# Three edits to a hybrid decoder-layer kernel: an earlier plain load, two other PSUM banks, and a norm in two parts

## The chip, the cores and the metric

The kernel runs on one core of a Trainium2 chip. The core has five engines that work side by side and wait for one another through semaphores: TensorE (PE, matmuls; its weight loads are shown as PEld), VectorE (DVE), ScalarE (ACT), GpSimd (POOL) and SyncE (SP, which issues transfers). Matmul results go to PSUM, which has 8 banks of 512 float32 columns on 128 partitions; everything else lies in SBUF. The metric is the device time of one execution, in microseconds (us). Each engine works its instructions off in order; a wait at the head of its queue holds back all that is behind it.

## The reference

One layer of a decoder is computed for a prompt of 1024 tokens and for 8 sample tokens with a paged cache. What matters here is branch B and the MLP:

```
h = RMSNorm(x);  z = h @ w_in                     # pool channels, q1 q2, k1 k2, v, gates
q, k = rope(q), rope(k)                           # 8 heads, two maps of 64 channels each
s = q k^T / 8, masked;  p = softmax(s)            # for each of the two maps
o = (p[0] - lam * p[1]) @ v                       # per head, 128 x 128 per token block
o = RMSNorm_head(o) * (1 - lam_init)
merged = gate_pool * (pool_out @ w_pool_proj) + gate_attn * (o @ w_attn_proj)
x = x + merged @ w_o
x = x + square(relu(RMSNorm(x) @ w_up)) @ w_down
y = RMSNorm(x)
```

All is float32; the kernel splits each operand of a large product into a high and a low part (`_hi`, `_lo`) and sums three products of those.

## The kernel before, in words

There is no scheduler: the order on each engine is written out, and semaphores are counted.

**Heads.** The 8 heads are pipelined. `head(h, ...)` exists once for each engine and runs nine steps s = 0 to 8 (NTT = 8 token blocks and one for the samples). In step s, TensorE computes the scores of block s of head h (`scores`, L853), sums the values of block s-2 (`values`, L895), projects token block s of the *next* head with one third each of q, k, v (`project`, L836, in two halves of 12 matmuls; the samples' one, s = 8, is L825 to L829), transposes the weights of block s-1 (`weight_transposes`, L885) and turns q and k of block s-1 of the next head (`qk_transposes`, L845 and L846, called the turn). ScalarE takes the exponentials (L1361) and copies the high parts out of PSUM (L1368, L1346, L1374); VectorE takes the maxima (L1837), weighs (L1847 to L1852), takes the low parts (L1859, L1829), applies the rotary factors and frees the projection's bank (`rotate`, L1821 to L1825), and makes the low halves of the next weights (`split_qkv`, L1780). POOL finishes the rotary sums (L2526, L2527) and raises the variances to the power -1/2 (`rstd_head`, L2542).

**Banks.** Projections use bank 0, only blocks 1 and 8 (the samples) use bank 3; both bank 3 and bank 5 are the second halves of the scores' two maps, used from block 4 on. The turn uses bank 6, which the weights' transposes of blocks 4 to 7 use too. So turn 7 waits until VectorE has read the last transposed weights out of bank 6 (`s_atlo`), and the projection of block 0 of the head after waits until the samples' projection has been read (`z_before`, `s_zfree`), though it writes another bank.

**Norm.** In step 1 of the next head VectorE waits for the squares of head h-1, writes `o_var` (L1870), waits for POOL's `o_rstd` and multiplies the whole head with it (L1872), and only then goes on to the low part of block 0 (L1859). The normed head is transposed in step 3 (`out_transposes`, L904).

**The last head** has no projection beside it; parts of the first product after the heads (`first_tile`, L1026, and `first_product`, L931) fill in from step 3 on.

**Down projection.** It runs in four spans of 28 blocks (4 pairs of 7 products); a block of the last span has 2 k-tiles (12 matmuls of 258 columns, L1171), the others 4. A table says at which block of a span each of the next span's seven inputs is loaded by ScalarE's queue (`NEXT_LOAD_AT`, L1598) and at which two blocks it is split (`NEXT_SPLIT_AT`; high part on ScalarE L1605, low part on VectorE L2335). After the last span comes `last_half`, products of one more input, the plain half (number PLAIN, `ff_plain_scratch`, twice the bytes of the others in the last span), which by the same table is loaded at block 6 of the last span and split at blocks 9 and 11. VectorE also makes the weights' low parts (L2189), the weights' sums (L2202 to L2208) and the additions into x (L2348, L2356), of which some free the accumulators in which TensorE goes on.

Of the kernel before, what the change touches and what calls it, by code (L numbers as in the profile page):

```python
# [18 lines left out]
NTT = SEQ // P  # L19
NCH = 3  # L20
CH = TOK // NCH
HEADS = 8
# [61 lines left out]
FIRST_SPLIT_AT = ((111, 112), (113, 114), (115, 116), (117, 118), (119, 120), (121, 122), (123, 124))  # L84
NEXT_LOAD_AT = (6, 12, 22, 23, 24, 25, 26)
NEXT_SPLIT_AT = ((9, 11), (15, 18), (25, 26), (26, 27), (28, 29), (30, 31), (32, 33))
Y_AT = {2: 8, 4: 7, 6: 6, 8: 5, 10: 4, 12: 3}
# [6 lines left out]
def need(eng, sem, value):  # L94

    if isinstance(value, int) and value <= 0:
        return
    eng.wait_ge(sem, value)


def decoder_layer(nc, ins, outs):
# [209 lines left out]
    with ExitStack() as ctx:  # L311
# [84 lines left out]
        def z_of(hp, t):  # L396

            if hp == 0:
                return first_z(t)
            return ps[:, 3] if t in (1, NTT) else bank_z  # L400

        def z_before(hp, t):

            before = {0: 0, 1: 0, 2: 1, NTT: 2}.get(t, t)
            return 9 * hp + before

        VS = 2
# [133 lines left out]
        for c in range(PLAIN + 1):  # L541
            g, i = divmod(c, W_BLOCKS)
            before = DOWN + W_BLOCKS * PER * (g - 1)
            load_at[c] = before + NEXT_LOAD_AT[i] if g else FIRST_LOAD_AT[i]
            split_at[c] = [before + k for k in NEXT_SPLIT_AT[i]] if g else FIRST_SPLIT_AT[i]

        def acc_a(p):
# [249 lines left out]
        def _(pe):  # L797
# [12 lines left out]
            def project(hp, t, half):  # L810
# [3 lines left out]
                if half == 0:  # L814
                    need(pe, s_zfree, z_before(hp, t) if hp else t - 1)
                    if hp and t == NTT:
                        pe.wait_ge(s_exp, 16 * hp)
                if hp and t == NTT:
                    if half == 0:
# [28 lines left out]
            def scores(h, par, i):  # L848

                pe.wait_ge(s_qklo, 8 * h + i + 1)  # L850
                need(pe, s_exp, 16 * h + 2 * (i - 1 if h == HEADS - 1 and 2 <= i <= 3 else i))
# [85 lines left out]
            def head(h, par, proj, normed):  # L937

                def turn_qk(t):

                    if t == 0:
                        need(pe, s_atlo, 12 * h)
                    elif t >= 4:
                        pe.wait_ge(s_atlo, 12 * h + ROUNDS[t] + 2)
                    else:
                        pe.wait_ge(s_qklo, 8 * (h + 1) + t)
                    if t == 2 and normed:
                        pe.wait_ge(s_one, 2 * h - 1)
                    qk_transposes(h + 1, 1 - par, t)

# [360 lines left out]
        def _(act):  # L1311
# [79 lines left out]
            def head(h, par, proj, normed):  # L1391
                if proj:
                    split_qkv(h + 1, (2, 3) if normed else (0, 1, 2, 3))
                for s in range(NTT + 1):
# [23 lines left out]
                    if proj and s >= 1:  # L1418
                        qk_high(h + 1, 1 - par, s - 1)
                    if proj and s == NTT:  # L1420
# [354 lines left out]
        def _(dve):  # L1775
# [91 lines left out]

            def normed_head(h, par):
                dve.wait_ge(s_oq, 8 * h + 8)
                dve.tensor_scalar(o_var[:], ssq[:, par], 1.0 / DH, SUBLN_EPS, ALU.mult, ALU.add).then_inc(s_ovar, 1)  # L1870
                dve.wait_ge(s_orstd, h + 1)
                dve.tensor_tensor(o_st[:, par], o_st[:, par], o_rstd[:].unsqueeze(2).to_broadcast([P, NTT, P]),  # L1872
                                  ALU.mult).then_inc(s_on, 1)

            def head(h, par, proj, normed, k_par):
                if proj:
                    split_qkv(h + 1, (2, 3) if normed else (0, 1, 2, 3))
                for s in range(NTT + 1):
# [5 lines left out]
                    if normed and s == 1:  # L1884
                        normed_head(h - 1, 1 - par)
                    if s >= 2:
# [18 lines left out]
                    if proj and s >= 1:  # L1905
                        qk_low(h + 1, 1 - par, s - 1)

# [75 lines left out]
            key_products(0)  # L1983
            o_sum(HEADS - 1, 1, NTT - 1)
            normed_head(HEADS - 1, 1)
            for s_ in s_kv:
# [639 lines left out]
```

## Time and profile before

| | us |
|---|---|
| median of 3 runs | 1711.28 (1711.20 to 1712.22) |
| the profiled execution's own time | 1712.73 |
| its span, first to last instruction | 1710.7 |
| busy: PE / DVE / ACT / POOL | 1667.7 / 1188.4 / 736.9 / 133.7 |
| mean granted TensorE clock | 0.993 of full |

The profile is of one execution. Busy times overlap between engines. In rows of the timeline a bracket gives how long the engine had been idle before the row, and what ended it; the ends of matmuls are modelled, so that the distance from start to start tells more than the idle time of PE.

### The profile page before, as it was taken

Reading aid. Unit: us, or ns where it says so; the run is one execution under the profiler, and the core shown is the slowest. Engines: PE = TensorE matmul, PEld = TensorE weight load, DVE = VectorE, ACT = ScalarE, POOL = GpSimd, SP = SyncE. Lnnn points to the kernel's source line nnn. Section 1 sums busy time; section 2 is a strip of 40 time slices with the busy share of each in tenths; the row PEclk is TensorE's granted clock in tenths of the full one; section 3 lists DMA queues with packets and bytes.
Section 4 is the critical chain, followed back from the end, with each engine's and each line's share of the span. In section 5 each row is a group of like instructions: output and inputs, shape, how many; then the busy total and the mean of one; then the engine's idle time right before and its main releaser. Section 6 shows DMA issues by size and latency. Waiting matters only on the chain.

```text
span 1710.7 us, 30509 instructions
## 1 busy us (share of the span) xinstructions
PE 1667.7 (97%) x12112; PEld 1614.6 (94%) x12112; DVE 1188.4 (69%) x1978; ACT 736.9 (43%) x1512; POOL 133.7 (8%) x244
## 2 busy tenths in 40 slices
PE   7999999999989999999999999999999999999988
PEld 7889889889878999999999999999999999999987
DVE  6677777777776788765444458777676786868686
ACT  4455555555554321265311345334433553544343
POOL 3212212222210000000000000000000000000001
PEclk9999999999999999999999999999999999999999
DMA  6202202201213527665412222444444733444223
GB/s 205 63 2 75 63 16 72 75 23 54 69 32 104 182 93 229 204 216 173 142 50 62 75 87 66 158 148 154 138 136 137 280 123 119 155 157 137 92 75 125
DMA packets 153212, 195.22 MB, mean 114 GB/s; under 512 B 7785, under 2 KB 121385, under 8 KB 151016
## 3 DMA queue, kind: packets, MB, share of 16 engines
q1 hardware_dynamic: 138352, 160.56, 29.4%
q10 hardware_dynamic: 14720, 32.72, 5.3%
q8 instruction: 97, 1.59, 0.4%
q14 instruction: 43, 0.35, 0.1%
HBM read 149.35 MB, written 44.13 MB: 113 GB/s over the span
## 4 chain that ended last, share of the span: by engine, by line
PE 89%; DVE 6%; issue 2%; ACT 2%; DMA 1%; POOL 0%; DVEq 0%; ACTq 0%; POOLq 0%
PE ps L1171 34%; PE ps L931 23%; PE ps L836 16%; PE ps L862 3%; PE ps L895 3%; PE ps L885 2%; PE ps L1224 1%; PE ps L1281 1%; PE ps L1078 1%; DVE kv_pages L1962 1%; DVE w_lo L1780 1%; PE ps L866 1%; DVE mx L1837 1%; PE ps L806 0%; DMA d_raw<-ff_plain_scratch 0%
## 5 line engine op out<-in xcount | busy, mean ns | idle before, releaser
L836 PE MATMUL ps<-w_hi,h_hi 128*128 128x384 f32 x520 | 182.3, 351 | 4.7 <-DVE w_lo L1780 2.7
L836 PE MATMUL ps<-w_hi,h_lo 128*128 128x384 f32 x520 | 176.8, 340 | 0.0
L836 PE MATMUL ps<-w_lo,h_hi 128*128 128x384 f32 x520 | 176.0, 338 | 0.0
L1171 PE MATMUL ps<-d_hi,m_hi 128*128 128x258 f32 x784 | 158.8, 284 | 5.3 <-DVE m_lo L2189 2.6
L1171 PE MATMUL ps<-d_lo,m_hi 128*128 128x258 f32 x784 | 159.2, 285 | 0.0
L1171 PE MATMUL ps<-d_hi,m_lo 128*128 128x258 f32 x784 | 158.2, 283 | 0.0
L1361 ACT ACTIVATE prob<-ps,nbias 128x256 f32<-128x256 f32 (+7 forms) x128 | 94.9, 742 | 84.8 <-DVE nbias L1840 82.4
L1171 PEld LDWEIGHTS ps<-d_hi,m_hi 128*128 128x128 f32 x784 | 121.6, 190 | 6.0 <-DVE x L2356 3.0
L1171 PEld LDWEIGHTS ps<-d_hi,m_lo 128*128 128x128 f32 x784 | 122.4, 190 | 0.0
L1171 PEld LDWEIGHTS ps<-d_lo,m_hi 128*128 128x128 f32 x784 | 121.8, 190 | 0.0
L1578 ACT ACTIVATE m_hi<-m_pair 128x512 fp32r<-128x512 f32 (+1 forms) x128 | 76.9, 600 | 104.3 <-PE ps L1171 91.5
L2189 DVE TENSOR_TENSOR m_lo<-m_pair,m_hi 128x512 fp32r<-128x512 f32 (+1 forms) x128 | 83.9, 655 | 50.6 <-ACT m_hi L1578 49.4
L1578 ACT ACTIVATE m_hi<-m_sum 128x512 fp32r<-128x512 f32 (+1 forms) x96 | 57.8, 602 | 112.1 <-PE ps L1171 85.0
L836 PEld LDWEIGHTS ps<-w_hi,h_hi 128*128 128x128 f32 x520 | 97.7, 188 | 7.4 <-DVE kv_st L1825 3.3
L1171 PE MATMUL ps<-t_hi,m_hi 128*128 128x258 f32 x512 | 104.0, 285 | 0.0
L1171 PE MATMUL ps<-t_lo,m_hi 128*128 128x258 f32 x512 | 103.8, 284 | 0.0
L1171 PE MATMUL ps<-t_hi,m_lo 128*128 128x258 f32 x512 | 103.8, 284 | 0.0
L931 PE MATMUL ps<-h_hi,w_hi 128*128 128x344 f32 x456 | 99.0, 326 | 3.7 <-DVE w_lo L1979 1.7
L1837 DVE TENSOR_REDUCE mx<-ps 128x1 f32<-128x256 f32 (+7 forms) x128 | 96.0, 750 | 7.6 <-PE ps L866 7.6
L1464 ACT ACTIVATE w_hi<-w_raw 128x1024 fp32r<-128x1024 f32 x42 | 44.4, 1057 | 129.5 <-PE ps L931 117.0
L836 PEld LDWEIGHTS ps<-w_lo,h_hi 128*128 128x128 f32 x520 | 98.1, 189 | 0.6
L836 PEld LDWEIGHTS ps<-w_hi,h_lo 128*128 128x128 f32 x520 | 97.5, 188 | 0.7
(295 smaller groups left out, 4335.7 us busy)
## 6 DMA issues: line engine op xcount, KB each, us to landing
ff_combination_scratch<-ff_st SPq DMA_DIRECT2D x14, 1806.0 KB, 6.9
d_raw<-ff_combination_scratch ACTq DMA_DIRECT2D x21, 1032.0 KB, 7.9
w_raw<-in_w_in SPq DMA_DIRECT2D x41, 512.0 KB, 5.3
kv_pages<-in_cache_k SPq DMA_DIRECT2D x32, 512.0 KB, 5.3
kv_pages<-in_cache_v SPq DMA_DIRECT2D x32, 512.0 KB, 4.5
m_pair<-in_w_up SPq DMA_DIRECT2D x16, 1024.0 KB, 9.6
m_pair<-in_w_down SPq DMA_DIRECT2D x24, 512.0 KB, 5.4
out<-kv_st SPq DMA_DIRECT2D x16, 512.0 KB
```

The source lines that it names most:

```text
L836: mm = pe.matmul(bank[0:n, 0:3 * P], a[:, kt, toks(t)], w[:, :, kt, :], start=(kt == 0 and m == 0), stop=(kt == KT - 1 and m == 2))
L862: pe.matmul(bank_s[:, c, o + 512 * b:o + 512 * b + n], q[part, par, 0, i * P:(i + 1) * P], k[part, par, 1, 512 * b:512 * b + n], start=(m ...
L866: pe.matmul(bank_s[:, c, o + i * P:o + (i + 1) * P], identb[:], mask[:], start=False, stop=True, skip_group_check=True).then_inc(s_s, 1)
L885: mm = pe.transpose(bank_t[r][:, (k - 4 * r) * P:(k - 4 * r + 1) * P], prob[:, i % 2, 0, k * P:(k + 1) * P], ident[:])
L895: mm = pe.matmul(bank_o[:, 0:2 * P], a[:, k * P:(k + 1) * P], v_hl[:, par, k].rearrange("p s e -> p (s e)"), start=(k == 0 and m == 0), st ...
L931: mm = pe.matmul(ps[:, SET[sp] + c, 0:CH], w, a[:, c * CH:(c + 1) * CH], start=(first and m == 0), stop=(last and m == 2))
L1171: mm = pe.matmul(acc[:, c], w[:, kt], a[:, kt % kts, c * CW:(c + 1) * CW], start=(opens and kt == 0 and m == 0), stop=(kt == n - 1 and m = ...
L1361: act.activation(prob[:, i % 2, c, 0:n], bank_s[:, c, o:o + n], ACT.Exp, bias=nbias[:, i % 2, c:c + 1], scale=SCALE, accum_out=sums[:, i, ...
L1464: act.activation(w_hi[:, lp], w_raw[:, lp], ACT.Copy).then_inc(s_whi, 1)
L1578: act.activation(weight_place(k)[0], weight_source(k), ACT.Copy).then_inc(s_mhi, 1)
L1837: dve.tensor_reduce(mx[:, i % 2, c:c + 1], bank_s[:, c, o:o + n], AX_X, ALU.max).then_inc(s_mx, 1)
L2189: dve.tensor_tensor(lo, weight_source(k), hi.bitcast(F32), ALU.subtract).then_inc(s_mlo, 1)
```

## The change

1. The plain half is loaded at block 1 of the last span (its second block) in place of block 6, and split at blocks 19 and 25 in place of 9 and 11.
2. The samples' projection goes to bank 5, turn 7 to bank 3. Turn 7 waits for the freeing of bank 3 in place of `s_atlo`; the projection of block 0 of the head after no longer waits for the samples' one. New waits are put where the banks are used again: before the projection of block 1 and before the scores of block 4 (block 2 in the last head).
3. `normed_head` is divided: `head_variance` stays where the whole was, the multiplication comes at the end of step 1, behind the low part of the turn (in the last head: behind the weights of block 1 and the low part of one weight).

```diff
+PLAIN_LOAD_AT, PLAIN_SPLIT_AT = 1, (19, 25)
...
-            return ps[:, 3] if t in (1, NTT) else bank_z
+            return ps[:, 3] if t == 1 else ps[:, 5] if t == NTT else bank_z
...
-            before = {0: 0, 1: 0, 2: 1, NTT: 2}.get(t, t)
+            before = {0: -1 if hp > 1 else 0, 1: 0, 2: 1, NTT: 2}.get(t, t)
...
+        def turn_bank(t):
+            return ps[:, 3] if t == NTT - 1 else bank_t[1]
...
+            if c == PLAIN:
+                load_at[c], split_at[c] = before + PLAIN_LOAD_AT, [before + k for k in PLAIN_SPLIT_AT]
...
+                    if hp and t == 1:
+                        pe.wait_ge(s_qklo, 8 * hp)
...
-                pe.wait_ge(s_qklo, 8 * h + i + 1)
+                pe.wait_ge(s_qklo, 8 * h + (NTT if i == (2 if h == HEADS - 1 else 4) else i + 1))
...
+                    elif t == NTT - 1:
+                        pe.wait_ge(s_zfree, z_before(h + 1, 2) + 1)
                     elif t >= 4:
                         pe.wait_ge(s_atlo, 12 * h + ROUNDS[t] + 2)
...
-                    qk_transposes(h + 1, 1 - par, t)
+                    qk_transposes(h + 1, 1 - par, t, turn_bank(t))
...
-                        qk_high(h + 1, 1 - par, s - 1)
+                        qk_high(h + 1, 1 - par, s - 1, turn_bank(s - 1))
...
-            def normed_head(h, par):
+            def head_variance(h, par):
                 dve.wait_ge(s_oq, 8 * h + 8)
                 dve.tensor_scalar(o_var[:], ssq[:, par], 1.0 / DH, SUBLN_EPS, ALU.mult, ALU.add).then_inc(s_ovar, 1)
+
+            def normed_head(h, par):
                 dve.wait_ge(s_orstd, h + 1)
...
                     if normed and s == 1:
-                        normed_head(h - 1, 1 - par)
+                        head_variance(h - 1, 1 - par)
...
-                        qk_low(h + 1, 1 - par, s - 1)
+                        qk_low(h + 1, 1 - par, s - 1, turn_bank(s - 1))
+                    if normed and s == 1:
+                        normed_head(h - 1, 1 - par)
```

The order on TensorE, POOL and SP is the same as before, only waits differ. On VectorE in step 1 of a head there stands before (`o_var`, `o_rstd`: variance and its power; `aT_lo`: low part of the transposed weights; `rc`, `rs`, `kv_st`: rotary products and v; `mx`: a maximum):

```order
L1870 TENSOR_SCALAR o_var<-ssq 128x8 [waits o_squares]
L1872 TENSOR_TENSOR o_st<-o_st,o_rstd 128x1024 [waits o_rstd]
L1859 TENSOR_TENSOR aT_lo<-ps,aT_hi 128x128 [waits wT_hi_ready]
L1847 RECIPROCAL rsum<-sums 128x2 [waits exp_ready]
L1849 SCALAR_TENSOR_TENSOR ratio<-sums,nlam,rsum 128x1 [waits rsum_ready]
L1852 SCALAR_TENSOR_TENSOR prob<-prob,ratio 128x256 [waits ratio_ready]
L1821 TENSOR_TENSOR rc<-ps,rope_c 128x256 [waits qk_rotated,z_ready]
L1823 TENSOR_TENSOR rs<-ps,rope_s 128x4x2x32
L1825 COPY kv_st<-ps 128x128
L1829 TENSOR_TENSOR qk_lo<-ps,qk_hi 128x2x128 [waits qk_hi_ready]
L1837 TENSOR_REDUCE mx<-ps 128x1 [waits scores_ready]
```

and after the change, in the same place of VectorE (lines are numbered 10 to 12 higher):

```order
L1880 TENSOR_SCALAR o_var<-ssq 128x8 [waits o_squares]
L1869 TENSOR_TENSOR aT_lo<-ps,aT_hi 128x128 [waits wT_hi_ready]
L1857 RECIPROCAL rsum<-sums 128x2 [waits exp_ready]
L1859 SCALAR_TENSOR_TENSOR ratio<-sums,nlam,rsum 128x1 [waits rsum_ready]
L1862 SCALAR_TENSOR_TENSOR prob<-prob,ratio 128x256 [waits ratio_ready]
L1831 TENSOR_TENSOR rc<-ps,rope_c 128x256 [waits qk_rotated,z_ready]
L1833 TENSOR_TENSOR rs<-ps,rope_s 128x4x2x32
L1835 COPY kv_st<-ps 128x128
L1839 TENSOR_TENSOR qk_lo<-ps,qk_hi 128x2x128 [waits qk_hi_ready]
L1884 TENSOR_TENSOR o_st<-o_st,o_rstd 128x1024 [waits o_rstd]
L1847 TENSOR_REDUCE mx<-ps 128x1 [waits scores_ready]
```

The multiplication has moved eight instructions back, between `qk_lo` and the maximum of step 2. On ScalarE in the last span there stands before, from block 4 to block 11 (`d_raw_189` and `d_hi_171` are the plain half's input and its high part, `m_hi` the weights' high parts, `part` an accumulator's copy):

```order
L1578 ACTIVATE m_hi_220<-m_sum 128x256 [waits mlp_products,mlp_w_sums]
L1598 DMA d_raw_189<-ff_plain_scratch 128x2064 [waits ff_stored0,mlp_products]
L1578 ACTIVATE m_hi_216<-m_sum 128x256 [waits mlp_products,mlp_w_sums]
L1637 ACTIVATE part_p_222<-ps 128x516 [waits down_added,mlp_products]
L1578 ACTIVATE m_hi_218<-m_sum 128x256 [waits mlp_products,mlp_w_sums]
L1637 ACTIVATE part_p_223<-ps 128x516 [waits down_added,mlp_products]
L1605 ACTIVATE d_hi_171<-d_raw_189 128x1032 [waits slot_in3]
L1578 ACTIVATE m_hi_220<-m_pair_169 128x256 [waits mlp_products,mlp_w_sums]
L1637 ACTIVATE part_u_228<-ps 128x516 [waits down_added,mlp_products]
L1578 ACTIVATE m_hi_216<-m_pair_169 128x256 [waits mlp_products,mlp_w_in1]
L1605 ACTIVATE d_hi_171<-d_raw_189 128x1032
```

After the change the load stands 10 instructions earlier on ScalarE, in front of the split of another input:

```order
L1647 ACTIVATE part_p_223<-ps 128x516 [waits down_added,mlp_products]
L1608 DMA d_raw_189<-ff_plain_scratch 128x2064 [waits ff_stored0,mlp_products]
L1615 ACTIVATE d_hi_178<-d_raw_196 128x516 [waits slot_in1]
L1588 ACTIVATE m_hi_218<-m_pair_168 128x256 [waits mlp_products,mlp_w_sums]
L1647 ACTIVATE part_u_228<-ps 128x516 [waits down_added,mlp_products]
```

The second low part stands on VectorE at block 25 now, between the last addition of a copy (`part_u`) and those of block 24's and 25's accumulators (`x<-ps`):

```order
L2363 TENSOR_TENSOR x_98<-part_u_228,x_98 128x516 [waits partial_out]
L2350 TENSOR_TENSOR d_lo_180<-d_raw_189,d_hi_171 128x1032 [waits combinations_hi]
L2371 TENSOR_TENSOR x_98<-ps,x_98 128x516 [waits down_added,mlp_products]
L2204 TENSOR_TENSOR m_lo_217<-m_pair_169,m_hi_216 128x256 [waits mlp_w_hi]
L2371 TENSOR_TENSOR x_98<-ps,x_98 128x516 [waits down_added,mlp_products]
L2204 TENSOR_TENSOR k_lo_198<-m_down_213,k_hi_197 128x512 [waits mlp_w_hi]
```

Before the change the same place was without the `d_lo` row.

## Rows read from the trace of the kernel before

**Rows 1.** Windows, one head: us, busy of each engine (instructions), clock, DMA share, GB/s
```profile
249.19:311.95 62.76, 62.24 (x429) 56.49 (x429) 47.28 (x119) 33.13 (x92) 14.72 (x27) 1.00 0.18 52
```
**Rows 2.** Waits of PE, 60 to 500 us: in total, times, longest
```profile
PE ps L836 <- DVE kv_st L1825: 2.1, 6, 0.4
...
PE ps L845 <- DVE aT_lo L1859: 1.0, 6, 0.2
```
**Rows 3.** Timeline of PE across a head's end: start, us, what, idle before
```profile
248.52 0.34 PE L829 MATMUL ps<-w_hi,h_samples 128*40 128x384 f32 x1
249.03 0.33 PE L845 MATMUL ps<-ident,q_nat 128*128 128x128 f32 x1 [0.17 <-DVE aT_lo L1859]
...
251.82 0.28 PE L895 MATMUL ps<-v_hl,aT_lo 128*128 128x256 f32 x1
252.45 0.44 PE L836 MATMUL ps<-w_hi,h_hi 128*128 128x384 f32 x1 [0.35 <-DVE kv_st L1825]
...
254.66 0.34 PE L836 MATMUL ps<-w_hi,h_hi 128*128 128x384 f32 x1
...
255.72 0.34 PE L836 MATMUL ps<-w_hi,h_hi 128*128 128x384 f32 x1
...
256.86 0.39 PE L862 MATMUL ps<-qk_hi 64*128 64x256 f32 x2
...
261.72 0.34 PE L836 MATMUL ps<-w_hi,h_lo 128*128 128x384 f32 x1
261.90 0.27 PE L845 MATMUL ps<-ident,q_nat 128*128 128x128 f32 x1
```
**Rows 4.** Timeline of DVE, ACT and POOL in the same stretch
```profile
252.66 1.81 DVE L1780 TENSOR_TENSOR w_lo<-w_raw,w_hi 128x768 fp32r<-128x768 f32 x2
...
261.12 1.23 DVE L1872 TENSOR_TENSOR o_st<-o_st,o_rstd 128x1024 f32<-128x1024 f32 x1 [1.76 <-POOL o_rstd L2542]
262.26 0.29 DVE L1859 TENSOR_TENSOR aT_lo<-ps,aT_hi 128x128 fp32r<-128x128 f32 x1
...
264.50 0.55 DVE L1837 TENSOR_REDUCE mx<-ps 128x1 f32<-128x384 f32 x1
...
255.54 0.19 ACT L1361 ACTIVATION_READ_ACCUMULATOR prob<-ps,nbias 128x1 f32 x1
...
252.48 2.30 POOL L2526 TENSOR_TENSOR qs_st<-rc,rs 8x128 f32<-8x128 f32 x1 [5.83 <-DVE kv_st L1825]
...
259.44 1.65 POOL L2542 TENSOR_TENSOR o_rstd<-o_var,half_neg 128x8 f32<-128x8 f32 x1
```
**Rows 5.** Timeline of ACT, DVE and POOL, steps 0 and 1 of the last head
```profile
507.38 0.26 ACT L1368 ACTIVATE aT_hi<-ps 128x128 fp32r<-128x128 f32 x1
...
508.92 0.28 DVE L1859 TENSOR_TENSOR aT_lo<-ps,aT_hi 128x128 fp32r<-128x128 f32 x1
...
503.63 0.44 POOL L2526 TENSOR_TENSOR qs_st<-rc,rs 8x128 f32<-8x128 f32 x1 [5.96 <-DVE kv_st L1825]
```
**Rows 6.** Windows, steps 2 and 3 of the last head (columns as rows 1)
```profile
507.50:517.70 10.20, 7.08 (x26) 5.71 (x27) 7.68 (x19) 4.07 (x13) 0.24 (x1) 0.50 0.44 124
```
**Rows 7.** Waits of PE in the last span and after, 1630 to 1675 us
```profile
PE ps L1171 <- DVE m_lo L2189: 2.6, 1, 2.6
...
PE ps L1171 <- DVE x L2356: 1.0, 1, 1.0
```
**Rows 8.** Chain that ended last, in the last span: start, us, what
```profile
1635.95 6.55 DMA d_raw<-ff_plain_scratch
```
**Rows 9.** Timeline of DVE and PE in the last span
```profile
1643.61 1.23 DVE L2335 TENSOR_TENSOR d_lo<-d_raw,d_hi 128x1032 fp32r<-128x1032 f32 x1 [2.86 <-ACT d_hi L1605]
...
1668.65 0.69 DVE L2356 TENSOR_TENSOR x<-ps,x 128x516 f32<-128x516 f32 x1
...
1661.11 0.40 PE L1171 MATMUL ps<-d_hi,m_hi 128*128 128x258 f32 x2
...
1669.75 0.41 PE L1171 MATMUL ps<-d_hi,m_hi 128*128 128x258 f32 x2
```

More of the change, by code:

```diff
@@ L1984, in _ @@
             o_sum(HEADS - 1, 1, NTT - 1)
+            head_variance(HEADS - 1, 1)
             normed_head(HEADS - 1, 1)
```

## Prediction, written before the run

> **What bounds the kernel now.** I read the engines' busy times first. In a head the window of 62.76 us has TensorE busy for 62.24 at the full clock, VectorE for 47.28 [rows 1]: heads are bound by TensorE's own work, and only what interrupts its stream, or slows its clock, can be won. So I then read its waits, and each one in the timeline from start to start. Two stand out in the heads, six times each: the first matmul of a projection waits for `kv_st`, and a turn for `aT_lo` [rows 2]. Behind the heads the waits of the last span show 2.6 us for `m_lo` and 1.0 for `x` in one place each [rows 7], and the chain that ended last passes through the transfer of the plain half, 6.55 us [rows 8].
>
> **Part 2, the banks, in heads 0 to 5.** Between the last matmul of the samples' projection and turn 7 lie 0.51 us from start to start (248.52 to 249.03); where a turn does not wait, as at 261.90, it is 0.18 [rows 3]. The wait for bank 6 costs 0.33. After the change the turn waits for bank 3, whose last reader (`kv_st` of block 1) is six steps back, so nothing takes its place. Projection of block 0 starts at 252.45, 0.63 behind the last matmul of the values at 251.82. Matmuls of 384 columns follow each other in 0.177 (six from 254.66 to 255.72, 1.06), those of 256 columns in two thirds of that, 0.12: 0.51 lost. The first 12 matmuls then take 2.21 (252.45 to 254.66) where 12 x 0.177 is 2.12: 0.09 more for starting anew [rows 3]. Together 0.33 + 0.51 + 0.09 = 0.93 a boundary.
>
> What is late next? The second half of this projection begins at 254.66 and 255.72 on low weights that VectorE makes in two instructions, together 252.66 to 254.47 [rows 3, 4]; by halves they are ready at about 253.6 and 254.5. With TensorE 0.93 earlier they are wanted at 253.7 and 254.8. The exponential of block 0 ends at 255.54 + 0.19 = 255.73 and the scores at 256.86 would then start at 255.93 [rows 3, 4]. So 0.1, 0.3 and 0.2 us are in hand, if VectorE and ScalarE stay where they are; they partly follow TensorE forward. The bounds for a boundary are 0 (something else was due at the same time) and 0.93; I take 0.93, because each of the three was measured as early enough. Six boundaries: **5.6 us**. The new waits (projection of block 1, scores of block 4) are for reads made at the end of the head before, a step or more back: nothing.
>
> **Part 3, the norm, in heads 1 to 6.** VectorE stands idle for 1.76 us behind POOL's `o_rstd` (259.44, 1.65 long), multiplies for 1.23 and only at 262.26 makes `aT_lo` [rows 4]. The turn of the same step starts at 261.90 and the values of block 0 follow behind it and the weights' transposes [rows 3]; `aT_lo` is just in time now and would be late with everything 0.93 earlier. After the split VectorE is free for it from 261.12 - 1.76 = 259.36. The multiplication counts 1.23 in its new place, before the maximum of step 2. That maximum stands at 264.50 [rows 4]; without the idle 1.76 VectorE could reach it at 262.7, and it is wanted at 264.50 - 0.93 = 263.6, 0.9 in hand. So part 3 is worth nothing here by itself; it is what keeps part 2's gain. Queued behind the multiplication's wait for POOL are the maximum, and through it the exponentials and TensorE's next scores; POOL is done by 261.1, before the wait is reached. Without that cover the wait would cost up to 1.76 a head.
>
> In the new order two small products of two SBUF inputs (`ratio`, `prob`) run beside `o_rstd`, where VectorE stood still. That the two engines disturb each other can be seen: POOL's `qs_st` of 8 x 128 takes 2.30 us beside the two `w_lo` instructions [rows 4] and 0.44 in the last head, where there are none [rows 5]. The Trainium skill ("SBUF — State Buffer", section "SBUF: two separate sides") says that a VectorE operation with two SBUF inputs and a GpSimd operation that reads SBUF share a port pair which is "an exclusive lock, not a bandwidth split", held for the whole instruction. By that, and the trace's 2.30 agrees with it (1.81 of `w_lo` plus about 0.44), `o_rstd` delays `ratio` and `prob` until 261.1 at the most and is itself delayed by one instruction at the most: the sum stays as it is. Stretching in proportion would be a rival, below.
>
> **The last head.** Turn 7 is released as in the others, 0.33 plus 0.06 for starting anew. Then `aT_lo` of block 0 stands at 508.92 because the norm is ahead of it, while its input `aT_hi` is there from 507.38 + 0.26 = 507.64 [rows 5]. TensorE has no projection to do in the meantime, so I count the difference less a handover of some 0.05 as won: 1.23, bounded by 0 (if the weights' sums behind it are the real limit) and 1.28. Together **1.6 us**. In the stretch behind it, 507.50 to 517.70, the clock is granted at 0.50, which is the 1.2 GHz level, with 7.08 of TensorE busy; the fall comes in this stretch, where it waits most [rows 6]. If the idle time that goes were enough to keep the clock up, half of 7.08, 3.5, would be won as well; if the low stretch grew as much, 3.5 would be lost. Of the 3.1 us that TensorE is idle there at most 1.2 go, so I take no change of the clock.
>
> **Part 1, the plain half.** Blocks of the last span follow each other every (1669.75 - 1661.11) / 6 = 1.44 us [rows 9]. Its transfer is issued at 1635.95, takes 6.55 [rows 8], then ScalarE's high part and at 1643.61 the low part, for which VectorE had been idle 2.86 [rows 9]; the `m_lo` behind it is what TensorE waits 2.6 for. The 1.0 for `x` comes two blocks later: the second `d_lo`, 1.23 long, stands before the addition that frees an accumulator [rows 7, 9]. At a boundary of heads 0.35 were shown idle [rows 3] and 0.60 were lost, so a stall costs some 0.25 more than is shown: 2.6 + 1.0 + 0.5 = 4.1. After the change the transfer is issued five blocks earlier, 7.2 us or more: by 1628.7, and with the same 6.55 it lands by 1635.3. It is needed at block 19, two before the one at 1661.11 [rows 9], over 20 us later: nothing waits for it. ScalarE's issue moves too, past one split and two weights' high parts, and costs neither of them anything, since it waits for products and a store long done.
>
> In their new places the low parts displace other work on VectorE. At block 19 the 1.23 falls between weights' parts that are wanted a block later: nothing, bounds 0 and 0.5. At block 25 it stands before the addition at 1668.65 (0.69 long), whose end at 1669.34 lets block 27 start at 1669.75 [rows 9]. The addition is late by 1.23 less the overlap of a following instruction (0.1) and VectorE's slack there (some 0.2), and block 27, which had 0.3 in hand over the usual handover, by 0.65 with its restart; bounds 0 and 0.92. Part 1 gives 4.1 - 0.7 = **3.4 us**, between 2.6 and 4.1.
>
> **Sum.** 5.6 + 1.6 + 3.4 = 10.6. The profiled execution took 1712.73, its span 1710.7, 2.0 outside it; that leaves 1702.1 for such an execution. The median of the runs, 1711.28, lies 1.45 below the profiled one, and my forecast is for the median: **1700.7 us**. Its own range, from the bounds without a change of mechanism, is 1699.5 to 1702.5.
>
> **Rivals.**
> (a) The clock keeps up in the last head. For it: less idle time in that stretch; against it: over half of the stretch's idle time stays. 1700.7 - 3.5 = 1697.2.
> (b) The boundary's wait only changes its name: the projection no longer waits for `kv_st` but for `w_lo` or, a little later, the scores for the exponential. For it: margins of 0.1 to 0.3; against it: VectorE also gets there earlier, since the turn does. The projection's 0.60 is given back, 6 x 0.6 = 3.6: 1704.3. If the turn's 0.33 goes too, because VectorE sets the pace of a head, 5.6 is lost: 1706.3. Against that: VectorE's 47.28 of 62.76 [rows 1].
> (c) The change does not do what it says: neither heads nor the last span gain, since VectorE's queue is what both wait for, and 5.6 and most of the 3.4 come back in other waits. 1709.5 to 1711. Against it: VectorE's idle times of 1.76 and 2.86 in just these places.
> (d) Slower: `o_rstd` is stretched by VectorE's small products as `qs_st` was, and by the same factor, 2.30 / 0.44 = 5.2, to 8.6 us. It ends at 268.0, the multiplication at 269.2, the maximum of step 2 is wanted at 263.6: 5.6 a head late, 34 in six: 1734. It costs anything only from an `o_rstd` of 263.6 - 1.23 - 259.4 = 2.9 us on, and turns the whole change to a loss from 4.7 on. Against it: what stood beside `qs_st` were two long instructions, here there are only a few on 1 or 256 elements a partition.
>
> **How the numbers follow.** Chances: forecast 0.66, (a) 0.08, (b) 0.12 at 1704.3 and 0.04 at 1706.3, (c) 0.06, (d) 0.04. The range from 1696.5 to 1705.5 holds all but (c), (d) and the second half of (b), 0.14. A measurement of this kernel can tell 0.2%, 3.4 us, from no change, that is below 1707.9 and above 1714.7: faster 0.90, same 0.06, slower 0.04.
>
> **What would show it.** In the trace after: PE's waits from 60 to 500 us have neither `kv_st` before a projection nor `aT_lo` before turn 7; a head's window is 0.9 shorter; VectorE has no idle before the multiplication; no new waits of PE for `w_lo` or `prob` at the boundaries (if they are there, it is (b)). In the last head `aT_lo` stands within 0.1 of its `aT_hi`. In the last span the waits of 2.6 and 1.0 are gone, and one of some 0.6 stands before block 27; the clock of steps 2 and 3 of the last head is still 0.50 (if not, (a)). An `o_rstd` above 2.9 us would make it (d). The forecast is wrong if a head's window is shorter by less than 0.6, or if what the last span gains is outside 2.6 to 4.1.

## The result, and the profile after

| kernel | median (runs) | lowest to highest | ratio to before, 95% interval |
|---|---|---|---|
| before | 1711.36 (4) | 1711.20 to 1712.22 | |
| changed | 1700.12 (4) | 1698.06 to 1701.12 | 0.9932 (0.9915 to 0.9949) |

The changed kernel is 11.2 us faster; 1700.7 was forecast. The profiled execution of it took 1699.59, with a span of 1697.5. TensorE issues the same 12112 matmuls in the same order in both, so their starts can be laid side by side (the aligned starts): each place where the distance between the two traces jumps is a place of gain or loss. A jump is counted here with the second or third matmul behind it, until the distance is steady again. From this the table of the whole span:

| place | jump in TensorE's starts, us | predicted |
|---|---|---|
| six boundaries: turn 7, and the projection behind it | 0.39 and 0.61 each, less 0.13 to 0.16 given back inside this and the next projection: 5.2 together | 5.6 |
| turn 7 ahead of the last head | 0.39 | 0.39 |
| low part of block 0 in the last head | 1.23 | 1.23 |
| last span, blocks 11 and 13 | 2.84 and 1.28 | 4.1 |
| last span, block 27 | -0.71 | -0.65 |
| sum of these | 10.2 | 10.6 |
| stretches at a low TensorE clock, where only one of the two has them, and waits that answer to them | 2.9 | 0 |
| first to last matmul | 13.15 | |

Of the 2.9, 1.6 belong to the two executions profiled and not to the change; of the other 1.4, in the last head, this stays open (below). The expectations below were written with jumps that I had read a little otherwise (0.87 a boundary, 0.3, 1.3, 2.76, 1.26 and 0.52); in sum they differ by 0.1.

The window of one head after the change, aligned with that of [rows 1] (columns: TensorE, its weight loads, VectorE, ScalarE, POOL, clock, DMA share, GB/s):

```profile
248.14:310.06 61.92, 61.92 (x431) 56.51 (x428) 47.53 (x119) 33.05 (x92) 15.72 (x27) 1.00 0.18 52
```
It is 0.84 shorter than the 62.76 of before, and shows TensorE with no idle time in it. The waits of TensorE from 60 to 500 us, all of them:

```profile
PE ps L844 <- DVE w_lo L1790: 2.1, 1, 2.1
```
The twelve waits of [rows 2] are gone; this one, a single wait, was there before as well. The weight loads have a new one, small and six times over (before the change there was none of this name):

```profile
PEld ps L844 <- DVE w_lo L1790: 1.0, 6, 0.2
```
The timeline of TensorE at the same head's end (start, length):

```profile
247.81 0.34 PE L837 MATMUL ps<-w_hi,h_samples 128*40 128x384 f32 x1
247.98 0.27 PE L853 MATMUL ps<-ident,q_nat 128*128 128x128 f32 x1
...
250.71 0.28 PE L903 MATMUL ps<-v_hl,aT_lo 128*128 128x256 f32 x1
250.83 0.34 PE L844 MATMUL ps<-w_hi,h_hi 128*128 128x384 f32 x1
```
0.17 and 0.12 from start to start, where [rows 3] had 0.51 and 0.63. The second half of this projection then waits 0.16 for its low weights (252.94), of which 0.10 is lost from start to start. VectorE and POOL in step 1 behind it:

```profile
259.08 0.29 DVE L1869 TENSOR_TENSOR aT_lo<-ps,aT_hi 128x128 fp32r<-128x128 f32 x1 [0.43 <-ACT aT_hi L1378]
...
259.73 0.48 DVE L1862 SCALAR_TENSOR_TENSOR prob<-prob,ratio 128x256 f32<-128x256 f32 x1
...
261.66 1.38 DVE L1884 TENSOR_TENSOR o_st<-o_st,o_rstd 128x1024 f32<-128x1024 f32 x1
262.96 0.55 DVE L1847 TENSOR_REDUCE mx<-ps 128x1 f32<-128x384 f32 x1
...
258.72 1.65 POOL L2557 TENSOR_TENSOR o_rstd<-o_var,half_neg 128x8 f32<-128x8 f32 x1
...
261.91 1.44 POOL L2542 TENSOR_TENSOR kv_st<-rc,rs 128x128 f32<-128x128 f32 x1
```
The low part waits for ScalarE alone; the multiplication finds `o_rstd` ready since 260.4, and the idle 1.76 of [rows 4] is gone. The maximum of step 2 stands 1.54 earlier than in [rows 4], but TensorE is 1.62 earlier here by all it has won up to this place: against TensorE the maximum comes 0.08 later than before.

In the last head, waits of TensorE from 499 to 525 us, and then the timeline of VectorE and ScalarE around the low part of block 0:

```profile
PE ps L893 <- DVE prob L1862: 2.4, 2, 1.4
PE ps L903 <- DVE aT_lo L1869: 1.8, 1, 1.8
PE ps L912 <- DVE aT_lo L1869: 0.7, 1, 0.7
```
```profile
503.14 0.29 DVE L1869 TENSOR_TENSOR aT_lo<-ps,aT_hi 128x128 fp32r<-128x128 f32 x1 [1.67 <-ACT aT_hi L1378]
...
501.89 1.04 ACT L1467 ACTIVATE w_hi<-w_raw 128x1024 fp32r<-128x1024 f32 x1
502.84 0.27 ACT L1378 ACTIVATE aT_hi<-ps 128x128 fp32r<-128x128 f32 x1
```
`aT_lo` now follows its input at once. VectorE is idle for 1.67 ahead of it, and ScalarE works on a weight meanwhile: the next bound has an address, which the last experiment uses.

In the last span, waits of TensorE, and then the timeline of VectorE and TensorE around block 27:

```profile
PE ps L1181 <- DVE d_lo L2350: 1.6, 1, 1.6
PE ps L1305 <- DVE x L2488: 0.6, 1, 0.6
PE ps L1181 <- DVE x L2371: 0.4, 1, 0.4
```
```profile
1653.58 1.23 DVE L2350 TENSOR_TENSOR d_lo<-d_raw,d_hi 128x1032 fp32r<-128x1032 f32 x1
1654.73 0.69 DVE L2371 TENSOR_TENSOR x<-ps,x 128x516 f32<-128x516 f32 x1
1655.34 0.41 DVE L2204 TENSOR_TENSOR m_lo<-m_pair,m_hi 128x256 fp32r<-128x256 f32 x1
1655.67 0.68 DVE L2371 TENSOR_TENSOR x<-ps,x 128x516 f32<-128x516 f32 x1
...
1656.41 0.51 PE L1181 MATMUL ps<-d_hi,m_hi 128*128 128x258 f32 x2 [0.44 <-DVE x L2371]
```
The waits of 2.6 and 1.0 of [rows 7] are gone. The new one of 0.44 stands before block 27, behind the second low part, as forecast; the other two (1.6 and 0.6) are in both kernels.

### The profile page after: what moved, and what is told of

It is laid out like the page before. It is cut to its first block, busy times and chain, and to the rows that moved or that the text cites. A ratio compares the mean times of both kernels' runs of the same rounds, so it can differ in the third digit from the quotient of the medians.

```text
span 1697.5 us, 30516 instructions
## 1 busy us (share of the span) xinstructions
PE 1660.1 (98%) x12112; PEld 1608.5 (95%) x12112; DVE 1189.3 (70%) x1978; ACT 736.8 (43%) x1512; POOL 139.5 (8%) x244
## 4 chain that ended last, share of the span: by engine, by line
PE 91%; DVE 5%; issue 2%; ACT 1%; SPq 0%; DMA 0%; POOL 0%; DVEq 0%; ACTq 0%
PE ps L1181 35%; PE ps L939 23%; PE ps L844 16%; PE ps L903 4%; PE ps L870 3%; PE ps L893 2%; PE ps L1234 1%; PE ps L1291 1%; PE ps L1088 1%; DVE kv_pages L1976 1%; PE ps L874 1%; DVE mx L1847 1%; PE ps L837 1%; PE ps L836 1%; PE ps L854 0%
```

## Which part gives what

Each run below was timed beside the kernel before on the same chip; a ratio is to that. Durations of single places are from the aligned starts.

**Part 1 alone** (only the table entry for the plain half):

> The kernel before with part 1 alone (plain half loaded at block 1, split at blocks 19 and 25). Theory: the last span's gain is independent of the heads. From start to start of TensorE's matmuls the changed kernel won 2.76 + 1.26 - 0.52 = 3.5 us there, so 1711.3 - 3.5 = 1707.8, the 2.6 and 1.0 waits gone and one of 0.4 before block 27. Rival (part of the tail's gain came from the heads, through the clock or the place of transfers): less than 2.5 gained.

Measured: 1707.88 (11 runs), ratio 0.9978 (0.9969 to 0.9987), that is 3.75 below the 1711.63 of before. The waits of the last span are those of the changed kernel (1.6, 0.6, 0.4), and from block 10 to the end of the span TensorE takes 26.40 us, 26.42 in the changed kernel and 29.83 before. The last span's gain does not need the heads.

How large it is depends on the execution of the old kernel that is taken. The plain half's transfer took 6.55 in the profile of before, 5.69 with part 2 alone and 6.80 with part 3 alone, and the same stretch 29.83, 28.97 and 30.09: a gain of 3.4, 2.6 and 3.7. The stall is longer or shorter by just what the transfer is. The forecast of 3.4 was made from one of these.

**Parts 2 and 3, without part 1:**

> The changed kernel without part 1 (plain half as before). Theory: six boundaries of 0.87 plus 0.3 for the seventh turn plus 1.3 in the last head is 6.8, so 1704.5. Rival (the clock's low stretches in the last head are shorter because of the heads' part): 1.5 to 3 more, 1701.5 to 1703.

Measured: 1705.40 (5 runs), ratio 0.9963 (0.9949 to 0.9976), 6.2 below, where the theory had 6.8; the rival's further 1.5 to 3 did not come. With 3.75 that makes 10.0: the two halves add up to the 10.2 of the table within what medians can tell.

**Part 2 alone**, the changed kernel with the norm whole in its old place:

```diff
                     if normed and s == 1:
                         head_variance(h - 1, 1 - par)
+                        normed_head(h - 1, 1 - par)
...
-                    if normed and s == 1:
-                        normed_head(h - 1, 1 - par)
```
and the lines of part 1 are taken out.

> The kernel before with part 2 alone, the norm whole in its old place. Theory as predicted (the split of the norm is what keeps the gain of the banks): TensorE's values of block 0 wait for aT_lo in every head, so that of the 0.87 a boundary only some 0.4 stays, 1711.3 - 2.4 - 0.3 = 1708.6. Rival (VectorE's chain itself comes 0.7 earlier with TensorE, so aT_lo is still in time): 5.2 + 0.3 stay, 1705.8, and only the last head's 1.3 is missing.

Measured: 1709.80 (11 runs), ratio 0.9994 (0.9985 to 1.0003): no difference that can be told. Waits of TensorE from 60 to 500 us, less the one that all kernels have, and then the timeline of VectorE and TensorE in step 1:

```profile
PE ps L901 <- DVE aT_lo L1867: 2.0, 6, 0.3
```
```profile
262.16 1.23 DVE L1882 TENSOR_TENSOR o_st<-o_st,o_rstd 128x1024 f32<-128x1024 f32 x1 [1.76 <-POOL o_rstd L2554]
263.31 0.28 DVE L1867 TENSOR_TENSOR aT_lo<-ps,aT_hi 128x128 fp32r<-128x128 f32 x1
...
263.64 0.38 PE L901 MATMUL ps<-v_hl,aT_hi 128*128 128x256 f32 x1 [0.33 <-DVE aT_lo L1867]
```
The boundary gives its 0.39 and 0.61, as in the changed kernel, and the same head takes them back: 0.10 in the projection itself, 0.53 where the values of block 0 wait for `aT_lo` at 263.64, and 0.36 a projection later. The waits have moved by a step, six of six. The theory stands, only that nearly all is given back and not half.

**Part 3 alone:**

> The kernel before with part 3 alone. Theory: nothing in heads 1 to 6, since no matmul waits for aT_lo there, and 1.2 to 1.3 in the last head, 1710.0. Rival (the moved multiplication delays the maxima): at or above 1711.3, with new waits of TensorE for exponentials.

Measured: 1708.89 (11 runs), ratio 0.9986 (0.9977 to 0.9995), 2.7 below, interval 0.9 to 3.9. The aligned starts show 0.06 a head lost in heads 1 to 6, at the projection of block 2, and 1.23 won in the last head: 0.9 in all, which lies at the edge of the interval. The rest to 2.7 has no place in the trace but low-clock stretches; that of the last head is 3.4 us shorter than before, which is worth 1.2 (below). So neither part 2 nor part 3 is worth anything in the heads before the last alone; together they are worth 5.2.

**The place of the multiplication.** The changed kernel, with the multiplication moved up directly behind the low part of block 0:

```diff
                         weight_low(h, s - 1, 0)
+                    if normed and s == 1:
+                        normed_head(h - 1, 1 - par)
...
                         qk_low(h + 1, 1 - par, s - 1, turn_bank(s - 1))
-                    if normed and s == 1:
-                        normed_head(h - 1, 1 - par)
```

> The changed kernel with the multiplication directly behind the low part of block 0 (aT_lo), so that VectorE waits there for POOL's o_rstd again, some 0.9 us at 259.5. Theory (the split gives its gain only because aT_lo no longer stands behind the wait): the maxima of step 2 come about 1.1 later, at 264.1, their exponentials end near 266.0 and TensorE's scores want them at 266.4, so nothing is lost: 1700.1, no new wait of TensorE from 60 to 500 us. Rival (the place behind the low part of the turn matters as well): 0.3 to 0.6 a head in a wait for exponentials or for the freed bank, 1702 to 1704.

Measured: 1706.25 (7 runs), ratio 0.9970 (0.9959 to 0.9981). The changed kernel has 1701.32 on another chip: 4.9 lost, and the theory with it; even the rival's 1702 to 1704 was too low. Waits of TensorE from 60 to 500 us, less that one, and then the timeline of VectorE and TensorE in steps 1 and 2 of one head:

```profile
PE ps L844 <- DVE kv_st L1835: 2.5, 6, 0.4
```
```profile
261.77 1.23 DVE L1884 TENSOR_TENSOR o_st<-o_st,o_rstd 128x1024 f32<-128x1024 f32 x1 [1.03 <-POOL o_rstd L2557]
...
269.60 0.28 DVE L1835 COPY kv_st<-ps 128x128 f32<-128x128 f32 x1
...
269.94 0.44 PE L844 MATMUL ps<-w_hi,h_hi 128*128 128x384 f32 x1 [0.41 <-DVE kv_st L1835]
```
The 1.03 of waiting for POOL is not wholly caught up before step 2 ends, and `kv_st`, the last reader of the projection's bank, comes late for TensorE's next projection: 0.60 to 0.68 a head, 3.9 in six, and 1.14 in the last head, where `prob` of block 1 now stands behind the multiplication. I had followed the maxima and the exponentials only, and not the other thing that stands behind on VectorE, the freeing of the bank.

## Load or split: what the last span's gain hangs on

Part 1 makes two edits, and the two were tried apart in the changed kernel.

```diff
-PLAIN_LOAD_AT, PLAIN_SPLIT_AT = 1, (19, 25)
+PLAIN_LOAD_AT, PLAIN_SPLIT_AT = 1, (9, 11)
```

> The changed kernel with the plain half loaded at block 1 but split at the old blocks 9 and 11. Theory (two causes: the 2.76 at block 11 was the late transfer, the 1.26 at block 13 the second low part ahead of an addition): the transfer's wait goes, the wait for x stays or moves to a neighbouring block, about 1.0 to 1.3 lost against the changed kernel, which has 0.4 to 0.5 of its own: 0.5 to 0.8 slower than the changed kernel, 1700.8. Rival (VectorE's queue behind the last splits of the seven inputs is the bound there): 2 or more slower, 1702 or above.

Measured: 1703.17 (5 runs), ratio 0.9951 (0.9937 to 0.9964). Waits of TensorE in the last span:

```profile
PE ps L1181 <- DVE d_lo L2350: 1.6, 1, 1.6
PE ps L1181 <- DVE x L2371: 1.0, 1, 1.0
PE ps L1305 <- DVE x L2488: 0.6, 1, 0.6
PE ps L1181 <- DVE m_lo L2204: 0.5, 1, 0.5
```
Aligned with the changed kernel it loses 0.71 at block 11 and 1.26 at block 13 and wins the 0.71 at block 27: 1.26. Of the 2.84 at block 11 the late transfer is therefore 2.13, and 0.71 was VectorE's first low part itself. The theory had the two causes right and the first of them too simple. The median lies in the range of the rival (1702 or above) and not at the theory's 1700.8, but the loss of 2 is not in the last span: this execution's trace has low-clock stretches at 528 and 733 us where the changed kernel's has none, and by the medians it loses 1.8 against the next run, timed on the same chip.

```diff
-PLAIN_LOAD_AT, PLAIN_SPLIT_AT = 1, (19, 25)
+PLAIN_LOAD_AT, PLAIN_SPLIT_AT = 6, (19, 25)
```

> The changed kernel with the plain half loaded at block 6 as before, split at blocks 19 and 25. Theory: the transfer is over long before block 19, so where it is issued is worth nothing once the splits are late: as the changed kernel, 1700.1. Rival (the load matters by itself, by its place on ScalarE's queue or beside other transfers): 1 us or more slower, 1701.1 or above.

Measured: 1701.34 (5 runs, 1698.16 to 1703.68), ratio 0.9940 (0.9927 to 0.9954). In its profile the transfer is issued 8.3 us later than in the changed kernel's (1617.88 there):

```profile
1626.19 0.34 ACTq L1608 DMA_DIRECT2D d_raw<-ff_plain_scratch  x1
```
and the last matmul starts 0.055 us from where it starts in the changed kernel, over the whole span. Where the splits are late, moving the load is worth nothing; the late splits alone do all of the 3.4. (With the splits in their old place the early load has the 2.13 of the transfer.) The median, 1701.34, is above the rival's 1701.1, but so is the changed kernel's own second one, 1701.32; the trace decides.

```diff
-PLAIN_LOAD_AT, PLAIN_SPLIT_AT = 1, (19, 25)
+PLAIN_LOAD_AT, PLAIN_SPLIT_AT = 1, (19, 22)
```

> The changed kernel with the second split at block 22 in place of 25, where VectorE stood idle 0.48 us and its next additions are of copies that free no accumulator TensorE wants at once. Theory: the wait for x before block 27 (0.44 shown, 0.52 from start to start) goes and nothing takes its place: 1699.6. Rival (the 1.2 us of VectorE only delays other additions): the same wait stands at another block, 1700.1 or above.

Measured: 1701.15 (5 runs), ratio 0.9942 (0.9929 to 0.9956). Timeline of ScalarE, VectorE and TensorE around block 24:

```profile
1647.90 1.06 ACT L1615 ACTIVATE d_hi<-d_raw 128x1032 fp32r<-128x1032 f32 x1
1648.85 0.41 ACT L1588 ACTIVATE m_hi<-m_sum 128x256 fp32r<-128x256 f32 x1
...
1648.98 1.23 DVE L2350 TENSOR_TENSOR d_lo<-d_raw,d_hi 128x1032 fp32r<-128x1032 f32 x1 [0.73 <-ACT d_hi L1615]
1650.14 0.42 DVE L2204 TENSOR_TENSOR m_lo<-m_sum,m_hi 128x256 fp32r<-128x256 f32 x1
...
1650.70 0.48 PE L1181 MATMUL ps<-d_hi,m_hi 128*128 128x258 f32 x2 [0.46 <-DVE m_lo L2204]
```
Block 27 wins 0.53 and block 24 loses 0.69: VectorE's idle time was there because ScalarE's high part was not, and the high part of the plain half makes that later still. The rival held.

## Further than both kernels

The last head's two moves, with the splits at 19 and 22:

```diff
+                    if not proj and s == 1:
+                        maximum(h, s + 1, 0)
+                        maximum(h, s + 1, 1)
                     if s >= 1:
                         weight_low(h, s - 1, 0)
...
-                    if not proj and s in (1, 2):
+                    if not proj and s == 2:
...
-                    if not proj and s in (1, 4):
+                    if not proj and s == 4:
                         high(s // 4)
...
                         o_squares(h - 1, 1 - par, NTT - 1)
+                    if not proj and s == 1:
+                        high(0)
```

> Split at 19 and 22, and in the last head the maxima of step 2 stand on VectorE ahead of the low part of block 0 (they would fill its 1.67 idle), and on ScalarE the high part of a weight (1.04) stands behind aT_hi of block 0. Theory: values of block 0 some 0.3 earlier, the weights of block 1 1.3 to 1.5 earlier, the later matmuls of the last head follow: 1.3 below the version with 19 and 22, 1698.3. Rival (the last head is bound by a chain through exponentials and sums that these do not shorten): same as the version with 19 and 22, 1699.6.

Measured: 1699.48 (5 runs), ratio 0.9928 (0.9914 to 0.9942), 1.7 below the version without the moves on the same chip (1.3 was forecast); between the matmuls 0.33 at the values of block 0 and 1.25 at the weights of block 1, of which 1.43 is left where the first product after the heads is under way.

The same with other places for the splits, 16 and 23:

> The last head as in the run with its maxima moved, and the plain half split at blocks 16 and 23: away from the additions that free accumulators, and behind the weights' high part that block 22 delayed. Theory: both the 0.6 before block 24 and the 0.5 before block 27 go, 0.6 below the version with 22: median 1699.0, lowest runs below 1697. Rival (VectorE has 2.3 us more to do in the last span wherever it stands, and one of its parts for TensorE is late by half of a us in any place): a wait of 0.4 to 0.6 stands at a third place and the last span takes as long as before.

Measured: 1701.36 (5 runs), ratio 0.9941 (0.9927 to 0.9954). Three jumps of 0.70, 0.33 and 0.70 at blocks 18, 20 and 25 against 0.38 won at block 27: 1.35 worse in the last span than 19 and 25. The theory failed, and the rival's one wait became three. Of the four pairs tried, (9, 11), (16, 23), (19, 22) and (19, 25), none is free of waits, and the last costs least: 27.69, 27.77, 26.58 and 26.42 us from block 10 to the end of the span.

At last the changed kernel and the two moves with the splits at 19 and 25, on one chip:

> The changed kernel once more, beside the next one on the same chip, for a comparison that does not go through another day's runs, and for the spread that TensorE's low-clock stretches give. Theory (the change removed 5.2 + 1.3 + 0.3 in the heads and 3.5 in the last span, the rest of any difference is where low-clock stretches fell): 1700 to 1702, 10 to 11 below the kernel before. Rival (part of the gain came from fewer low-clock stretches, for good): 12 or more below.

> The changed kernel with only the last head's two moves (maxima of step 2 ahead of the low part of block 0, a weight's high part behind aT_hi). Theory: the 1.7 that stood between the matmuls of the earlier run with these moves are kept to the end, 1.5 below the changed kernel beside it. Rival (a low-clock stretch takes the place of the idle time in the last head): within 0.5 of the changed kernel.

Measured: 1701.32 (0.9947, 0.9933 to 0.9960) and 1698.20 (0.9931, 0.9917 to 0.9944), five runs each, beside 1710.78 for the kernel before. The changed kernel is 9.5 faster here where it was 11.2 the first time; the rival, 12 or more, is out. VectorE of the latter in step 1 of the last head:

```profile
500.44 0.56 DVE L1849 TENSOR_REDUCE mx<-ps 128x1 f32<-128x384 f32 x1 [0.18 <-PE ps L874]
...
501.76 0.28 DVE L1871 TENSOR_TENSOR aT_lo<-ps,aT_hi 128x128 fp32r<-128x128 f32 x1
...
502.40 0.48 DVE L1864 SCALAR_TENSOR_TENSOR prob<-prob,ratio 128x256 f32<-128x256 f32 x1
```
The maxima fill the idle 1.67. At the weights of block 1 TensorE is 1.6 earlier than its neighbour for it (0.33 and 1.26), 1.5 of it is left after the heads, and the medians differ by 3.1; as the runs of each spread over 2.4 to 2.9 us, the 1.5 is what is shown. The low-clock stretch of the last head is shorter as well here (3.4 us in place of 6.8), and what of the 1.5 is due to that was not separated. This version has the lowest median of all that ran; by the ratios (0.9931 here, 0.9928 with 19 and 22, 0.9932 for the changed kernel the first time) the three can't be told apart.

## Why the prediction was right

The bound was read rightly: TensorE's own work in the heads, and what interrupts it.

- **A boundary, 0.93 forecast, 0.84 in the window, 0.84 to 0.87 in the aligned starts.** The turn's 0.33 and the projection's 0.51 came as forecast, each with its new start (0.06, which my sum has only in the last head, and 0.10). What brings it below 0.93 is that 0.10 is given back at once: I had put the margin of the first low weights at 0.1, and they come 0.1 too late. `w_lo` behind the samples starts at 251.95, 0.71 before its old place, and 0.72 is just what TensorE had won before this boundary: VectorE stayed where it was in the head, and rival (b) is there six times, as a sixth of its size. Its 0.6 is excluded. Another 0.03 to 0.06 go at the projection of block 2, which the split alone costs as well.
- **The norm as cover.** That the split earns nothing in heads 1 to 6 and keeps all was the forecast; part 2 alone and part 3 alone show it. What I put at up to 1.76 a head without it measured 0.84 (wait and multiplication ahead of the low part) and 0.64 (behind it). The 0.9 that I had in hand for the maximum of step 2 was not there: I took all 1.76 of idle time off, and 0.43 of it came back as a wait for `aT_hi` and 0.24 as one for the projection, and the multiplication took 0.15 longer. That the maximum 0.08 late cost nothing was luck as far as my account goes: the slack lies behind it. With the multiplication behind the low part it came another 0.6 late, and still no matmul waited for an exponential.
- **Rival (d)**, the stretched `o_rstd`: 1.65 before and after, `prob` 0.48 before and after. Excluded.
- **The last head.** 0.39 + 1.23, both as forecast.
- **The last span.** 4.12 against 4.1 for the two stalls, 0.71 against 0.65 for block 27, in the place named. The reading of it was half right: the load's new place, which I described at length, does nothing beside the late splits, and 0.71 + 1.26 of the 4.12 are VectorE's low parts and not the transfer. And it is luck that the sum fits so closely: with the transfers of two other profiles the same change gives 2.6 and 3.7.
- **The clock of the last head.** I took no change, and named a clock of 0.50 in steps 2 and 3 as the sign. It held in part: the low stretch is there, but shorter. After the change, first the low stretch itself, then what answers to 507.50 to 517.70 of [rows 6]:

```profile
502.10:508.90 6.80, 4.06 (x15) 2.69 (x16) 5.62 (x13) 3.38 (x10) 1.10 (x1) 0.50 0.63 172
502.10:510.50 8.40, 5.66 (x25) 4.29 (x26) 7.08 (x19) 4.61 (x13) 1.10 (x1) 0.60 0.64 180
```
with part 1 alone, which leaves the heads as they were, and with part 2 alone, which leaves the last head's norm as it was:

```profile
507.20:517.50 10.30, 6.90 (x25) 5.53 (x26) 7.68 (x19) 4.36 (x14) 0.53 (x1) 0.50 0.47 131
508.90:515.70 6.80, 4.52 (x17) 3.16 (x18) 5.77 (x15) 2.66 (x9) 0.00 (x0) 0.50 0.46 129
```
The shorter stretch is worth 1.2 to 1.4 in the aligned starts. It does not need the idle time that goes with the norm, since part 2 alone has it, so rival (a)'s reason is not the one, and its 3.5 did not come. But the two profiles with the heads unchanged have 10.3, and every one with part 2 or part 3 in it has 6.9 or less: whether the 1.4 is chance or the change's is open. Besides this, before has a low stretch at 535 to 538 that after lacks; the 1.4 that it costs is given back by 548, where TensorE waits for exponentials.

The 1.0 by which the median moved more than the 10.2 of the table is of this kind, and no run tells chance from the change in it. At a mean granted clock of 0.995 the kernel before took 1709.1 to 1711.9 (five of 27 runs, 1710.7 on the mean) and the changed one 1700.65 and 1701.12: 9.8 us apart. And the forecast of 1700.7 came as close as this because 0.4 too much in the heads stands against 1.0 that I had not counted.

## What to carry to other kernels

A wait that is taken off the bounding engine pays only if what stands next on the engine it waited for can come earlier too: here two edits that were each worth nothing in the heads before the last were worth 5 us together. Before reading "earlier" off a second trace, take off what the bounding engine has won up to that place. When an instruction is delayed, follow every result behind it on its engine, the freeing of a bank as much as the data. And where an edit has a load and a use in it, try the two apart before the load gets the credit.

## What was not expected of the hardware

- TensorE's clock falls to half in short stretches at places that differ between executions, and each costs 1.2 to 1.5 us. The kernel before has two while TensorE is busy without a break (columns as above):

```profile
739.40:743.40 4.00, 4.00 (x18) 4.00 (x18) 3.92 (x3) 0.91 (x4) 0.00 (x0) 0.57 0.86 239
1036.50:1041.00 4.50, 4.50 (x28) 4.46 (x28) 3.59 (x7) 3.31 (x6) 1.43 (x1) 0.62 0.00 0
```
  The changed kernel has neither (1.00 in both places), but one at 65 us that the kernel before lacks. The run with the early load and the old splits, which is the changed kernel up to the last span, has none at 65, but two at 528 and 733 us. 27 runs of the kernel before spread from 1707.5 (clock 0.997) to 1714.5 (0.991). An edit of one us can't be told by medians of five; it can by the aligned starts.
- When VectorE and POOL meet, POOL is the one that waits long. Its sum `kv_st` takes 0.46 elsewhere and 1.44 when it starts 0.25 behind the multiplication, ending 0.3 after it; where the multiplication stands behind the low part and no longer beside it, `kv_st` takes 0.46 again. The multiplication takes 1.38 where it took 1.23; POOL's `q_nat` (261.49, 0.46) was under way when it started. POOL's `qs_st` starts 0.19 ahead of the two `w_lo` and still takes 2.31, while these take their usual 1.8. And `o_rstd` (258.72 to 260.37) delays neither `ratio` nor `prob` (259.73, 0.48), though it began first: this is against the rule of the Trainium skill ("SBUF — State Buffer", section "SBUF: two separate sides") that whichever starts first holds the lock for its whole instruction, by which they would have been kept until 260.37. The measurement decides. That one of the two is blocked until the other is done is what the rows of `qs_st` and `kv_st` show, which end 0.3 behind VectorE's instructions; but `qs_st` was the first to start, here as in [rows 4], so the agreement that the prediction saw there is one of the length and not of the order.
